# Expert outputs accumulated in three tables instead of two, with separate ordering for each table

## The reference

```python
    def run_block(args):
        xblk, e = args
        hid = jax.nn.silu(xblk @ w1[e]) * (xblk @ w3[e])
        return hid @ w2[e]

    yb = lax.map(run_block, (xb, blk_e))
    routed = jnp.zeros((T, Dm), F32).at[tok_buf].add(yb.reshape(cap, Dm).astype(F32) * w_buf[:, None])
    shared = (jax.nn.silu(t @ ws1) * (t @ ws3)) @ ws2
    return (routed + shared.astype(F32)).astype(h.dtype).reshape(B, L, Dm)
```

## Time and profile before

| | |
|---|---|
| median of three runs | 1558.5 us |
| the profiled execution, its own time | 1560.39 us |
| span of that execution, first to last instruction | 1558.5 us |
| PE busy | 1441.4 us, 92% of the span |
| DVE busy | 834.4 us, 54% |
| POOL busy | 494.0 us, 32% |
| HBM read and written | 323.10 MB and 62.13 MB |
| mean granted TensorE clock | 0.964 of full speed |

### The profile page before, as it was taken

The page is one execution under the profiler, slowest core; times in us unless marked ns, Lnnn a source line. Parts: engine busy times, 40 slices in busy tenths (PEclk is TensorE's granted clock), DMA queues, the critical chain, the costliest instruction groups (busy, mean ns, idle before and its releaser), DMA issues.

```text
span 1558.5 us, 17507 instructions
## 1 busy us (share of the span) xinstructions
PE 1441.4 (92%) x5847; PEld 642.7 (41%) x5847; DVE 834.4 (54%) x2114; ACT 217.6 (14%) x369; POOL 494.0 (32%) x426
## 2 busy tenths in 40 slices
PE   4899999999999999989989999999989999999956
PEld 2344454555545554543423334433323333333312
DVE  1048678999989898856233233324333333333327
ACT  1111322313121322322000000000000000000003
POOL 0001010111213121225354555555454454555410
PEclk9899999999999999988799999999989999999988
DMA  9978202212121001412889999999999999999976
GB/s 328 330 301 308 84 28 97 70 41 84 41 71 41 17 31 43 141 71 65 306 283 364 375 358 385 370 364 315 381 369 338 384 368 362 336 323 327 365 218 279
DMA packets 93436, 364.69 MB, mean 234 GB/s; under 512 B 18965, under 2 KB 30649, under 8 KB 68207
## 3 DMA queue, kind: packets, MB, share of 16 engines
q1 hardware_dynamic: 69383, 304.29, 50.5%
q0 software_dynamic: 23968, 59.35, 15.2%
HBM read 323.10 MB, written 62.13 MB: 247 GB/s over the span
## 4 chain that ended last, share of the span: by engine, by line
DMA 40%; PE 25%; DVE 20%; issue 8%; SPq 4%; ACT 1%; POOL 0%; POOLq 0%; DVEq 0%; ACTq 0%
DMA acc_rows<-W,kT 19%; DMA acc_rows<-xr,kT 14%; PE U L655 9%; DVE cv L1263 8%; PE R L708 6%; DMA acc_rows<-xr,shared_f 4%; PE U L865 3%; SPq L404 2%; DMA W<-in_w_ada 2%; DMA x_t<-h_rows,q_r 1%; PE R L881 1%; PE R L619 1%; SPq L411 1%; PE T L672 1%; PE U L814 1%
## 5 line engine op out<-in xcount | busy, mean ns | idle before, releaser
L655 PE MATMUL U<-W,hT 128*128 128x512 f32 x864 | 386.7, 601 | 1.2 <-issue 1.2
L1263 DVE SCALAR_TENSOR_TENSOR cv<-win,cw,cv 128x128 f32<-128x128 f32 x960 | 254.9, 347 | 1.4
L865 PE MATMUL U<-W,hT 128*128 128x512 f32 (+2 forms) x784 | 236.8, 611 | 6.0 <-issue 6.0
L881 PE MATMUL R<-W,glu 128*32 128x512 f32 (+2 forms) x1024 | 240.9, 597 | 1.3 <-DVE glu L1555 1.3
L655 PEld LDWEIGHTS U<-W,hT 128*128 128x128 f32 x864 | 163.0, 194 | 189.1 <-issue 189.1
L865 PE MATMUL U<-W,cat 128*32 128x512 f32 (+2 forms) x1264 | 236.2, 603 | 0.0
L1542 DVE STREAM_TRANSPOSE hT<-x_t 128x1024 f32<-128x1024 f32 x33 | 67.3, 2040 | 195.6 <-DMA x_t<-h_rows,q_r 160.2
L1542 DVE STREAM_TRANSPOSE cat<-W 128x1024 f32<-128x1024 f32 x33 | 67.7, 2051 | 192.8 <-DMA W<-h_rows,q_r 192.8
L1742 POOL DMA_INDIRECT W<-h_rows,q_r x128 | 129.1, 1009 | 55.8 <-issue 55.8
L881 PEld LDWEIGHTS R<-W,glu 128*32 128x32 f32 (+2 forms) x1024 | 83.9, 138 | 151.4 <-issue 149.9
L865 PEld LDWEIGHTS U<-W,hT 128*128 128x128 f32 (+2 forms) x784 | 90.9, 158 | 128.1 <-issue 126.8
(11 more groups left out here) (295 smaller groups left out, 1178.2 us busy)
## 6 DMA issues: line engine op xcount, KB each, us to landing
W<-in_w SPq DMA_DIRECT2D x192, 1024.0 KB, 15.9
W<-in_w_ada SPq DMA_DIRECT2D x24, 1024.0 KB, 8.5
W<-in_w_in SPq DMA_DIRECT2D x6, 2048.0 KB, 19.8
W<-acc_rows SPq DMA_DIRECT2D x16, 512.0 KB, 10.4
h_rows<-xr SPq DMA_DIRECT2D x9, 512.0 KB, 2.7
x_t<-in_x_prompt SPq DMA_DIRECT2D x8, 512.0 KB
W<-in_w_out SPq DMA_DIRECT2D x1, 4096.0 KB, 17.6
xr<-in_x_prompt SPq DMA_DIRECT2D x8, 512.0 KB
```

The source lines that it names most:

```text
L655: last = mm(U[BANK[g]][:, :], hT[:, k, :], w_in[:, k, 512 * g:512 * g + 512], start=k == 0, stop=k == KT - 1)
L865: last = mm(U[1][cols, :], xgT[z][:, k, cols], w13[:, :, k, :], start=k == 0, stop=k == KT - 1)
L881: last = mm(R[cols, 512 * half:512 * half + 512], hidT[:, f, cols], weights[:, at:at + 512], start=f == 0, stop=f == FT - 1)
L1263: ins = v.scalar_tensor_tensor(cv[:, c, :], win[:, c, w:w + P], cw[:, c, w:w + 1], cv[:, c, :], ALU.mult, ALU.add)
```

## The change

A third table is added, and each table is a tensor of its own. `chains()` decides at build time, for every block, where its rows go: the two experts of a mixed block go to tables 0 and 1 in two DMAs, and a block of one expert, or of the shared expert, goes in one DMA to the table that is free first by an assumed 11 us for a block and for a scatter. `DONE[x][c]` counts the DMAs of table c up to block x. A scatter waits only for the earlier scatters of its own table. `blk_y(x)` waits for all DMAs up to block x - 2, in three waits. Rows that a DMA must leave out get an index far out of range (`skips()`). The tables are zeroed by three DMAs in each of the five passes instead of two. In the tail there are three loads for each tile, 6 `mm` for a sum on PE instead of 4, and one more addition on DVE for tile 0 and for the sample rows. All 66 blocks give 94 scatters: 36 to table 0, 33 to table 1 and 25 to table 2.

```diff
-NOWHERE = 4 * TABLE
+def pieces(x):
+    u = EXEC[x][0]
+    owners = [None] * 4 if u is None else [s for s, _ in QUARTERS[4 * u:4 * u + 4]]
+    first = owners.count(owners[0])
+    return [(0, first)] + [(first, 4 - first)] * (first < 4)
+
+
+def chains():
+    parts, done, busy = [], [], [0, 0, 0]
+    for x in range(NX):
+        cut = pieces(x)
+        tables = [min((2, 0, 1), key=lambda c: busy[c])] if len(cut) == 1 else [0, 1]
+        taken = [(c, at, n) for c, (at, n) in zip(tables, cut)]
+        for c, _, n in taken:
+            busy[c] = max(busy[c], 11 * x) + 11
+        parts.append(taken)
+        done.append(tuple(sum(c == table for block in parts for table, _, _ in block) for c in range(3)))
+    return parts, done
...
-        acc_there = [16 + 32, 16 + 32] + [16 + 64] * (TP - 2)
+        acc_there = [16 + 48, 16 + 48] + [16 + 96] * (TP - 2)
...
-        acc_rows = scratch("acc_rows", (2 * TABLE, D))
+        acc_rows = [scratch(f"acc_rows{i}", (TABLE, D)) for i in range(3)]
...
-                for x in range(2):
-                    sp.dma_start(acc_rows[bass.ds(i * 2 * P + TABLE * x - 4 * P, 2 * P), :], t["zeros"]).then_inc(spare_in, 16)
+                for x in range(3):
+                    sp.dma_start(acc_rows[x][bass.ds(i * 2 * P - 4 * P, 2 * P), :], t["zeros"]).then_inc(spare_in, 16)
...
+            sp.dma_start(third_s, in_pieces(acc_rows[2][SEQ:TOKENS, :])).then_inc(sample_in, 16)
             for i in range(TP):
...
+                sp.dma_start(third_t[i], acc_rows[2][P * i:P * i + P, :]).then_inc(acc_in[i], 16)
...
-                    for x in (acc_t[i], odd_t[i]):
-                        last = mm((X, R)[i % 2][:, half], ident[:, :], x[:, half], start=x is acc_t[i], stop=x is odd_t[i])
+                    for x in (acc_t[i], odd_t[i], third_t[i]):
+                        last = mm((X, R)[i % 2][:, half], ident[:, :], x[:, half], start=x is acc_t[i], stop=x is third_t[i])
...
-                dve.wait_ge(scattered[x % 2], 16 * (x // 2))
+                for c in range(3):
+                    if x > 1 and DONE[x - 2][c]:
+                        dve.wait_ge(scattered[c], 16 * DONE[x - 2][c])
...
-            v.tensor_tensor(slot_i[:, 0:NU], X[:, 0:NU], slot_base, ALU.add).then_inc(slot_ready, 1)
+            v.tensor_tensor(slot_i, X[:, 0:NU].unsqueeze(1).to_broadcast([P, 3, NU]), slot_base, ALU.add).then_inc(slot_ready, 1)
...
+                    link(v.tensor_tensor(acc_t[i], acc_t[i], third_t[i], ALU.add))
...
-                at = shared_i[:, 4 * NT + n:4 * NT + n + 1] if u is None else slot_i[:, u:u + 1]
                 pool.wait_ge(y_evac, x + 1)
-                if x > 0:
-                    pool.wait_ge(scattered[1 - x % 2], 16 * ((x + 1) // 2))
-                pool.indirect_dma_start(acc_rows, bass.IndirectOffsetOnAxis(ap=at, axis=0), y_sbs[x % 2], None,
-                                        bounds_check=2 * TABLE - 1, oob_is_err=False,
-                                        compute_op=ALU.add).then_inc(scattered[x % 2], 16)
+                before = [0, 0, 0] if x == 0 else list(DONE[x - 1])
+                for c, first, n in PARTS[x]:
+                    if before[c]:
+                        pool.wait_ge(scattered[c], 16 * before[c])
+                    before[c] += 1
+                    at = shared_i[:, 4 * NT + EXEC[x][1]:4 * NT + EXEC[x][1] + 1] if EXEC[x][0] is None else slot_i[:, c, EXEC[x][0]:EXEC[x][0] + 1]
+                    pool.indirect_dma_start(acc_rows[c], bass.IndirectOffsetOnAxis(ap=at, axis=0), y_sbs[x % 2], None,
+                                            bounds_check=TOKENS - 1, oob_is_err=False,
+                                            compute_op=ALU.add).then_inc(scattered[c], 16)
...
+def skips():
+    far = np.full((P, 3, NU), 8.0 * TABLE)
+    for x, (u, _) in enumerate(EXEC):
+        if u is not None:
+            for c, at, n in PARTS[x]:
+                far[32 * at:32 * at + 32 * n, c, u] = 0.0
+    return far.reshape(P, 3 * NU)
```

More of the change, by code:

```diff
@@ L101 @@
     free[r] = LAST[s]
+def pieces(x):
[14 more added lines that the diff above has]
+    return parts, done
+PARTS, DONE = chains()
 USE = tuple(SLOT[:s + 1].count(SLOT[s]) for s in range(NE))
@@ L180, in build @@
         more_in, more_ready, rounds_known = sem("more_in"), sem("more_ready"), sem("rounds_known")
-        gathered, scattered = ([sem(f"{n}{r}") for r in range(2)] for n in ("gathered", "scattered"))
+        gathered, scattered = ([sem(f"{n}{r}") for r in range(count)] for n, count in (("gathered", 2), ("scattered", 3)))
         def scratch(name, shape, dt=F32):
@@ L222, in build @@
         odd_t = [W[:, WE + (TP + 1 + i) * D:WE + (TP + 1 + i) * D + D] for i in range(TP)]
+        third_t = [W[:, WE + (TP + 2 * 0 + 1 + TP + i) * D:WE + (2 * TP + 1 + i) * D + D] for i in range(TP)]
+        third_s = W[:, WE + TP * D + 2 * SW:WE + TP * D + 3 * SW]
         odd_s = W[:, WE + TP * D + SW:WE + TP * D + 2 * SW]
@@ L581, in _ @@
                 sp.dma_start(g_s[rows], t["g_final"].rearrange("(c n) -> c n", n=SW)).then_inc(sample_in, 16)
[L582 removed]
+            sp.wait_ge(scattered[0], 16 * DONE[-1][0] + 16 * NE * rounds)
             sp.sem_inc(sp_free, 1)
[L584 to L587 removed]
+            sp.wait_ge(scattered[1], 16 * DONE[-1][1])
+            sp.wait_ge(scattered[2], 16 * DONE[-1][2])
+            sp.dma_start(acc_s, in_pieces(acc_rows[0][SEQ:TOKENS, :])).then_inc(sample_in, 16)
+            sp.dma_start(odd_s, in_pieces(acc_rows[1][SEQ:TOKENS, :])).then_inc(sample_in, 16)
+            sp.dma_start(third_s, in_pieces(acc_rows[2][SEQ:TOKENS, :])).then_inc(sample_in, 16)
             for i in range(TP):
[L589 to L590 removed]
+                sp.dma_start(acc_t[i], acc_rows[0][P * i:P * i + P, :]).then_inc(acc_in[i], 16)
+                sp.dma_start(odd_t[i], acc_rows[1][P * i:P * i + P, :]).then_inc(acc_in[i], 16)
+                sp.dma_start(third_t[i], acc_rows[2][P * i:P * i + P, :]).then_inc(acc_in[i], 16)
             for i in range(TP):
@@ L1657, in _ @@
             dve.wait_ge(x2_in, 16 * (TP + 2))
-            dve.wait_ge(sample_in, 16 * 20)
+            dve.wait_ge(sample_in, 16 * 21)
             link(v.tensor_tensor(acc_s, acc_s, odd_s, ALU.add))
+            link(v.tensor_tensor(acc_s, acc_s, third_s, ALU.add))
             link(v.tensor_tensor(acc_s, acc_s, gt_s, ALU.mult))
@@ L1794, in _ @@
                         pool.sem_inc(pool_free, 1)
-                        pool.indirect_dma_start(acc_rows, bass.IndirectOffsetOnAxis(ap=slot_cur, axis=0), y_sbs[0], None,
-                                                bounds_check=2 * TABLE - 1, oob_is_err=False,
+                        pool.indirect_dma_start(acc_rows[0], bass.IndirectOffsetOnAxis(ap=slot_cur, axis=0), y_sbs[0], None,
+                                                bounds_check=TOKENS - 1, oob_is_err=False,
                                                 compute_op=ALU.add).then_inc(scattered[0], 16)
@@ L1827, in constants @@
     base = every(LCAP * e + 1.0)
-    spare = np.where(token < TOKENS, token, NOWHERE)
+    spare = np.where(token < TOKENS, token, TOKENS + np.arange(P)[:, None])
     by_quarter = spare.reshape(4, 32, NT)[:, np.arange(P) % 32].transpose(1, 0, 2)
@@ L1835, in constants @@
         "rope": np.stack([cos, -sin, sin], 1), "blk_no": i[:, None], "quart": (i // 32)[:, None] / 4,
-        "list_base": base, "list_pad": np.tile(np.stack([NOWHERE + 0.0 * entry, 0.0 * entry], 1), (NE, 1)), "toks": token,
+        "list_base": base, "list_pad": np.tile(np.stack([TOKENS + entry % P, 0.0 * entry], 1), (NE, 1)), "toks": token,
         "dcol": np.concatenate([LCAP // 32 * i[:, None], np.resize([q for _, q in QUARTERS], 2 * P).reshape(2, P).T,
@@ L1840, in constants @@
         "zeros": np.zeros((2 * P, D)),
-        "slot_base": np.array([[TABLE * (QUARTERS[4 * u + p // 32][0] % 2) for u in range(NU)] for p in range(P)]),
+        "slot_base": skips(),
         "disp": np.concatenate([every(NE - 1.0 - e), every(np.resize([LINE[x] for x, _ in QUARTERS], 2 * P)), every(LINE), every(CAPS), base], 1),
     }
+def skips():
[5 more added lines that the diff above has]
+    return far.reshape(P, 3 * NU)
 OUTS = {
```

15 lines of the change are left out of this document (8 added, 7 removed).

## The result

The changed kernel took 1587.1 us (median of four runs, 1585.1 to 1594.5), the kernel before beside it 1559.2: a ratio of 1.020, interval 1.017 to 1.022.

The account below looks back on a forecast made before the run. Chained scatters were taken to pace blocks only 0.1 to 0.6 us above PE, with DMA the third resource. 1560.4 + 14 + 0.2 - 12 = 1562.6 us profiled, or 1560.7 against the 1558.5 median (+2.2); 8-in-10 range 1551 to 1570.

Parts of the forecast that it names:

- The tail: After the blocks: six table loads and sums of twelve matmuls cost 14 us more, bounds 11 and 17.
- a later wait: In the tail: loads for tiles 2 and 3 land about 1532.7, PE ready at 1531.5, so 1 us more.
- The padding rows are skipped as before, so no bytes are added to the blocks: Scatters in the blocks: skipped rows add no bytes, costed at nothing.
- There the gather comes 0.9 us earlier: Mixed blocks on POOL: scatter issued 2.8 us earlier, second scatter costs 1.61 and 0.3 us, leaving the gather 0.9 us earlier.
- Rival B: Mixed blocks: the second scatter makes gathers late, gain only 6 us, time 1566.5 us; chance 0.12.
- Blocks 15 to 26: Stage of one expert: 116 to 117 us instead of 122.4, at most 6.6 us gained, 6 taken.
- So this stage is had: Blocks 15 to 26: the DMA can carry the quicker pace, its queue growing only 2 us in the stage.
- my bound was 4: Blocks 26 to 38: gain taken as 0, with -4 us allowed for a longer queue at the start and +3 above.
- Rival A: All blocks: transfers are the bound, gain 5 to 7 us, time 1566.5; sign: blocks 26 to 38 over 147 us; chance 0.22.
- Blocks 38 to 65: Two last stages: 1 us gained in blocks 38 to 49 and 2 us in blocks 49 to 65.
- no stretch can be quicker than 11.03 us a block: All 66 blocks before: each scatter waits for the last, 10.15 us of landing and 0.88 us until POOL runs on.
- the lower end of the gain: All blocks: about 1 us if mixed blocks gain nothing, half the second stage is had and the third loses 4.

Follow-up runs that it names:

- own rows only: The changed kernel with a mixed block's two scatters each cut to its own expert's rows, 128 between them: 1573.4 us, ratio 1.0101.
- one-DMA version: The changed kernel with a mixed block's rows added to tables 0 and 1 in one indirect DMA, three tables ordered by table: 1567.9 us, ratio 1.0053.
- the tail alone: The kernel before with a third table zeroed, loaded and summed but never added to: 1573.4 us, ratio 1.0089.

## Why the prediction was wrong, step by step

- **The tail: right.** +14 forecast, 14.0 measured, 14.6 by itself. Sums take 5.15 us apiece, and the last scatters cost nothing, as assumed. One part was right by a balance: the first sum begins 11.4 us after the first table load instead of 7.6, 3.9 more, where I had 2.8, and the 1 us that I had for a later wait did not come (the second sum waits 0.2 us). The timeline of the tail after, against the earlier trace rows:

```profile
1524.16 0.35 SPq L612 DMA_DIRECT2D W<-acc_rows  x1
...
1535.60 7.31 PE L1009 MATMUL R<-W,ident 128*128 128x512 f32 x12 [22.66 <-DMA W<-acc_rows]
...
1569.09 5.31 PE L1009 MATMUL R<-W,ident 128*128 128x512 f32 x12
```

- **"The padding rows are skipped as before, so no bytes are added to the blocks": wrong, and the largest error.** I had looked for bytes to be added where the cost was rows to be skipped. Skipping 128 more rows in each of 28 blocks costs 13.7 us by the medians of the changed kernel and of own rows only. I had put this at nothing and named no cover for it.
- **"There the gather comes 0.9 us earlier":** the arithmetic of POOL's time was right, and it was beside the point. The gather's issue can be 1.6 us later at no cost. Rival B had the right sign, place and condition (transposition more than 8 us after `up`: it is 9.45); its price of 6 us was less than half of the 13.7, and its mechanism, POOL's issue, was refuted. The sign that scatters start about 0.9 us after their output did come true: over blocks 15 to 26 it is 0.8 us in every block, from 3.6 in the mean before. So the change did what it was to do, and its cost came from elsewhere.
- The Trainium skill (DMA: Bandwidth & Descriptors, Rules for kernel authors) has it that two transfers to disjoint partition halves serialise and one over 128 partitions is to be used. Cut to their own rows, the two scatters cost the blocks nothing here (293.0 against 292.7 us); the loss was in the skipped rows, of which that rule says nothing.
- **Blocks 15 to 26: right** in size, 117.1 us for 116 to 117. **"So this stage is had": wrong.** Its 5.3 us are set off by 2.2 lost in the stage before, which has five mixed blocks (with own rows only it gains 2.1 instead), and 3.1 in the stage after. In the one-DMA version, which gained 8.6 us by block 26, blocks 26 to 38 took 8.7 us longer; my bound was 4. From a queue that drains at 375 GB/s in one stage I had concluded that the transfers had room, where the whole of blocks 4 to 38 is what a weight waits for. Rival A was right for this half of the blocks and not for the other. Its sign, over 147 us for blocks 26 to 38, was missed by a hair in the changed kernel (146.7) and is plain in the one-DMA version (152.2).
- **Blocks 38 to 65:** the forecast of 3 us was right for the order by table (3.3 to 5.4 us with one DMA per block) and was overrun by the skipped rows.

Two statements of the prediction were wrong without changing its outcome. That no stretch can be quicker than 11.03 us a block while every scatter waits for the one before: the landing has no fixed length, and with fewer weights the kernel before ran blocks 4 to 38 at 10.8 us each with all these waits. And the lower end of the gain, "about 1": its terms come to -1 us. The measured gain in the blocks, -9 us, lies far below either.

Against the forecast of +2.2 us, the failure of the first half is 9 us and that of the second, with its own 3 us of gain, 12. With the forecast's 2.2 and the 1.8 us ahead of block 4 that makes the profile's 24.8, to 0.2. That start differs by several us between versions which do the same there (794.3 to 802.3), so I give it no cause; with the tail alone, zeroing of the third table included, block 4 starts at 798.9, as before (799.0). The medians differ by 28 us, 3 more than the two profiled executions.

## What to carry to other kernels

A row that an indirect DMA skips is not free: keep one transfer where its rows are all wanted, or cut each to the rows it needs, instead of sending the rest out of range, and look at packets, not bytes. Where loads run ahead in a ring, a stage's gain counts only if what must be loaded up to the next forced stop allows it; compare the mean rate over all of it, not the best stretch. And before removing a wait by splitting a resource, try a finer order on the resource as it is: here it brought a gain without the price.

## What the runs showed of the hardware that was not expected

- A DMA that adds rows, given 128 indices out of range: 144 packets in the queue (128 for the rows), and over 28 of them 14.7 MB in the written bytes, with no row added.
- A gather issued 1.6 us later behind the same scatter had its rows there at the same time, 15.5 us after the scatter against 15.6.
- On POOL a 128x512 subtraction started 1.08 us after the 1.61 us issue of an indirect DMA began, so the two overlap; it took 1.61 us there.
- The share of busy DMA engines says little of room: it is 0.99 at 355 GB/s and 0.98 at 328 GB/s, when PE waits for nothing.
- The Trainium skill (DMA: Bandwidth & Descriptors, Specifications) gives about 358 GB/s from HBM for a core. This kernel's mean over 389 us, 355, lies near it, but it is no ceiling for the one core that is used here: 375 GB/s held for 123 us. The same page of the Trainium skill says under Bandwidth, Measured, that about 358 is what each of two cores gets when both stream.
